# Four feed-forward networks on one core: another order of VectorE's adds and rests, and another order of work at the four entries

## The reference, cut to what matters

```
def swiglu_ffn(x, w_gate, w_up, w_down):
    return (jax.nn.silu(x @ w_gate) * (x @ w_up)) @ w_down
x = layer_norm(ALPHA * x + swiglu_ffn(x, ...), ln_ffn_g[l], ln_ffn_b[l])      # ffn0, ffn1

def sq_relu_mlp(h, w_up, w_down):
    u = jax.nn.relu(h @ w_up)
    return (u * u) @ w_down
h = h + sq_relu_mlp(rmsnorm(h, ln_mlp[layer]), w_up[layer], w_down[layer])    # mlp0, mlp1
```

## Time and profile before

| what | us |
|---|---|
| median of 3 runs | 2432.76 |
| the profiled execution, whole | 2433.45 |
| its span, first to last instruction | 2431.7 |
| TensorE busy | 2359.3 (97%) |
| VectorE busy | 1821.4 (75%) |
| ScalarE busy | 1144.4 (47%) |
| granted clock of TensorE, mean over the span | 0.991 of full speed |

### The profile page before, as it was taken

The page is one execution under the profiler, slowest core; times in us unless marked ns, Lnnn a source line. Parts: engine busy times, 40 slices in busy tenths (PEclk is TensorE's granted clock), DMA queues, the critical chain, the costliest instruction groups (busy, mean ns, idle before and its releaser), DMA issues.

```text
span 2431.7 us, 36017 instructions
## 1 busy us (share of the span) xinstructions
PE 2359.3 (97%) x13582; PEld 2023.7 (83%) x13582; DVE 1821.4 (75%) x2660; ACT 1144.4 (47%) x1846; POOL 24.8 (1%) x43
## 2 busy tenths in 40 slices
PE   8999999999999999999999999989999999899998
PEld 7887888899998887899998786778888777788887
DVE  6997646888777746888778636688888786888887
ACT  4455545444444744444445525444344565444443
POOL 0000000000000000000000000000000000000000
PEclk9999999999999999999999999999999999999999
DMA  5232313223223212223322220234422312223221
GB/s 182 104 139 87 121 35 104 89 102 103 103 89 147 97 43 70 93 98 103 103 93 102 87 104 18 88 100 121 120 97 99 122 53 70 71 102 103 99 91 70
DMA packets 39409, 232.56 MB, mean 96 GB/s; under 512 B 8901, under 2 KB 8981, under 8 KB 12560
## 3 DMA queue, kind: packets, MB, share of 16 engines
q1 hardware_dynamic: 31680, 219.17, 26.3%
q0 software_dynamic: 7632, 12.05, 1.7%
HBM read 223.80 MB, written 7.34 MB: 95 GB/s over the span
## 4 chain that ended last, share of the span: by engine, by line
PE 69%; DVE 17%; issue 8%; ACT 4%; DMA 1%; DVEq 1%; SPq 0%; ACTq 0%
PE bank L804 68%; DVE xs L2442 2%; DVE w_lo L2542 2%; DVE w_lo L2356 2%; DVE mhl L2595 2%; ACT w_hi L1651 1%; ACT xs L1732 1%; DMA w_raw<-weights_in 1%; ACT xh L1670 1%; DVE lox_y L2545 1%; DVE fhl L2595 1%; DVE tf_y L2628 1%; DVE cacc L2801 1%; DVE lox_x L2545 1%; PE bank L1582 1%
## 5 line engine op out<-in xcount | busy, mean ns | idle before, releaser
L804 PE MATMUL bank<-xh,w_hi 128*128 128x512 f32 (+1 forms) x1088 | 398.5, 366 | 22.9 <-DVE w_lo L2542 8.9
L804 PE MATMUL bank<-xh,w_lo 128*128 128x512 f32 (+1 forms) x1088 | 393.1, 361 | 0.0
L804 PE MATMUL bank<-xl,w_hi 128*128 128x512 f32 (+1 forms) x1088 | 393.1, 361 | 0.0
L2442 DVE TENSOR_TENSOR xs<-xs,bank 128x512 f32<-128x512 f32 x448 | 292.6, 679 | 38.8 <-PE bank L804 35.5
L2356 DVE TENSOR_TENSOR w_lo<-w_raw,w_hi 128x2048 fp32r<-128x2048 f32 x80 | 183.1, 2288 | 127.8 <-ACT w_hi L1651 127.7
L804 PEld LDWEIGHTS bank<-xh,w_hi 128*128 128x128 f32 x1088 | 208.2, 191 | 63.5 <-DVE w_lo L2542 9.8
L804 PEld LDWEIGHTS bank<-xl,w_hi 128*128 128x128 f32 x1088 | 208.7, 192 | 30.6 <-issue 0.5
L804 PEld LDWEIGHTS bank<-xh,w_lo 128*128 128x128 f32 x1088 | 208.4, 192 | 30.8
L804 PE MATMUL bank<-mhh,w_hi 128*128 128x512 f32 x512 | 204.7, 400 | 24.2 <-DVE mhl L2595 16.9
L2569 DVE TENSOR_TENSOR w_lo<-w_raw,w_hi 128x1024 fp32r<-128x1024 f32 x104 | 123.0, 1221 | 116.3 <-ACT w_hi L1798 116.3
L1810 ACT ACTIVATE rb<-bank 128x256 f32<-128x256 f32 x272 | 104.1, 383 | 220.0 <-PE bank L804 217.8
(11 more groups left out here) (383 smaller groups left out, 5781.1 us busy)
## 6 DMA issues: line engine op xcount, KB each, us to landing
w_raw<-weights_in SPq DMA_DIRECT2D x204, 1024.0 KB, 4.8
rel_scratch<-vt POOLq DMA_DIRECT2D x8, 384.0 KB, 19.4
bias<-rel_scratch POOLq DMA_DIRECT2D x8, 256.0 KB, 3.9
y_out<-xs SPq DMA_DIRECT2D x8, 256.0 KB, 2.2
xs<-x_in SPq DMA_DIRECT2D x3, 512.0 KB, 8.3
mk<-mem_in POOLq DMA_DIRECT2D x1, 1024.0 KB, 9.0
mem_kept<-memh POOLq DMA_DIRECT2D x1, 1024.0 KB, 4.3
mem_kept<-meml POOLq DMA_DIRECT2D x1, 1024.0 KB, 7.4
```

Source lines behind the costliest of these rows:

```text
L804: return pe.matmul(dst, a, b, start=start, stop=stop, skip_group_check=shared)
L2442: free(dve.tensor_tensor(xs[:, k, :], xs[:, k, :], bank(key)[:, :], ALU.add), key)
```

## The change

VectorE beside a down unit: each add goes ahead of the piece that it stood behind, adds 2 and 3 go ahead of piece 2, add 4 ahead of piece 3, the rests of the hidden chunk go behind piece 3, and in ffn the next unit's sums go behind adds 5 to 7. This runs in every call of beside_down.

At ffn's entry: the activation sums are made in the order in which seven uses them and split in that order, in between the pieces of gate 1; seven waits for each of them where it uses it; scale_residual goes to the end of the entry; the tile sums of gate 1 go ahead of pieces 1 to 3 of up 1, and ScalarE's order follows; the whole up unit goes to banks 4 and 5.

At mlp's entry: half_y is made by ScalarE straight behind the residual, ahead of the root; three of the four activation sums are made by VectorE ahead of the root and of unit 1's rests, the fourth behind these; the rests of two of the four and the sums of unit 3 go behind the rests of hidden chunk 0; the copy of the relative bias (L3205) and the wait for the root go into the entry, behind the sums.

```
@@ plan_banks: chunks
-            put(plain_up(name, "p0", "u", up_unit(name, 0), 2))
+            put(plain_up(name, "p0", "u", up_unit(name, 0), 4))
@@ TensorE: seven
                     if first:
-                        pe.wait_ge(sem["t_lo"], t_base[name] + 4)
+                        pe.wait_ge(sem["t_lo"], t_base[name] + 2)
                     free_bank("P2")
...
+                    if first:
+                        pe.wait_ge(sem["t_lo"], t_base[name] + 3)
                     product("R", r_[:, 0:MEM], of_unit(3), combined(2), start=True)
...
+                    if first:
+                        pe.wait_ge(sem["t_lo"], t_base[name] + 4)
                     product("P3", p_[:, 0:MEM], of_unit(2), combined(3))
@@ ScalarE
+            def scaled_tiles(gain):
+
+                for k in range(4):
+                    last = act.activation(half_y[:, k, :], xs[:, k, MEM:], ACT.Copy, scale=col(gain, k))
+                give(last, "scaled_half")
+
...
-                def combined_hi():
-
-                    for j in (0, 3, 1, 2):
+                def combined_hi(js=range(4)):
+
+                    for j in js:
...
-                    combined_hi()
+                    g1, u1 = gate_unit(name, 1), up_unit(name, 1)
+                    combined_hi((0, 1))
+                    quad(g1, 0)
+                    combined_hi((2, 3))
                     for m in range(2):
                         key = (name, "p0", "g", m)
                         drain(key, sil[:, m, :], bank(key)[:, :], ACT.Silu)
-                    for piece in range(4):
-                        quad(gate_unit(name, 1), piece)
+                    for piece in (1, 2, 3):
+                        quad(g1, piece)
+                    partial("p1", "g", "P1", 0)
+                    quad(u1, 0)
+                    partial("p1", "g", "Q1", 0)
                     for m in range(2):
                         hidden(0, m)
-                    beside_gate("p1", 1)
+                    partial("p1", "g", "P2", 0)
+                    quad(u1, 1)
+                    partial("p1", "g", "R", 0)
+                    for piece in (2, 3):
+                        quad(u1, piece)
+                    for m in range(2):
+                        silu("p1", 1, m)
...
             residual(pair_keys("go"), UNITS["go"], 4, None, gain="mlp2_g0")
+            scaled_tiles("mlp2_g0")
             rms_stats("r1")
@@ VectorE: sums_of_tokens (ffn) makes t1, t2, t4, t3 in this order; sums_of_scaled_tokens (mlp):
+                for j in js:
+                    if j == 0:
+                        g = COL[gain]
+                        steps.step(dve.tensor_scalar(ngain[:, :], prm[:, g:g + 4], -1.0, None, ALU.mult))
+                        steps.wait()
+                        seen.next("scaled_half")
+                        from_tiles(0, lambda k: xs[:, k, early], lambda k: ngain[:, k:k + 1], half, ALU.add)
...
+                    if j == 3:
+                        from_tiles(3, lambda k: xs[:, 4 + k, late], lambda k: col(gain, 4 + k), half, ALU.subtract)
@@ VectorE: beside_down
+                    adds(tag, (0,), i)
                     quad(n, 0, i)
-                    adds(tag, (0,), i)
+                    adds(tag, (1,), i)
                     quad(n, 1, i)
-                    rests(chunk, 0, i)
-                    adds(tag, (1,), i)
+                    adds(tag, (2, 3), i)
                     quad(n, 2, i)
-                    rests(chunk, 1, i)
-                    adds(tag, (2,), i)
+                    adds(tag, (4,), i)
                     quad(n, 3, i)
-                    adds(tag, (3, 4), i)
+                    for m in range(2):
+                        rests(chunk, m, i)
+                    adds(tag, (5, 6, 7), i)
                     if after is not None:
                         sums_of(after, i)
-                    adds(tag, (5, 6, 7), i)
@@ VectorE: entry of ffn
-                    combined_sums()
-                    sums_of(gate_unit(name, 1))
+                    g1, u1 = gate_unit(name, 1), up_unit(name, 1)
+                    sums_of_tokens()
+                    sums_of(g1)
+                    quad(g1, 0)
                     if name == "ffn0":
                         dve.wait_ge(mem_stored, 2 * 16)
-                    combined_lo()
-                    scale_residual()
-                    for piece in range(4):
-                        quad(gate_unit(name, 1), piece)
+                    combined_lo((0,))
+                    quad(g1, 1)
+                    combined_lo((1, 2))
+                    quad(g1, 2)
+                    quad(g1, 3)
+                    combined_lo((3,))
...
-                    sums_of(up_unit(name, 1))
+                    sums_of(u1)
+                    quad(u1, 0)
+                    sum_unit("p1", "g", 0)
+                    for piece in (1, 2, 3):
+                        quad(u1, piece)
                     for m in range(2):
                         rests(0, m)
-                    beside_gate("p1", 1)
+                    scale_residual()
@@ VectorE: entry of mlp
                     split_lo(U + 1)
-                    combined_sums()
-                    combined_lo()
+                    sums_of_scaled_tokens(gain, (3,))
+                    if name == "mlp0":
+                        key = ("vec", 0)
+                        wait_full(dve, key)
+                        free(dve.tensor_scalar(vt[0:16, 0:384], bank(key)[0:16, 0:384], -1.0, None, ALU.mult), key)
+                    combined_lo((0, 1))
+                    seen.next("rstd_ready")
                     first_hidden("p0", 0)
                     split_lo(U + 2)
-                    sums_of(up_unit(name, 2))
                     for m in range(2):
                         rests(0, m)
+                    combined_lo((2, 3))
+                    sums_of(up_unit(name, 2))
                     first_hidden("p1", 1)
...
             residual(pair_keys("go"), UNITS["go"], 4, False, gain="mlp2_g0")
-            key = ("vec", 0)
...
-            seen.next("rstd_ready")
+            sums_of_scaled_tokens("mlp2_g0", (0, 1, 2))
             chunks("mlp0", False)
```

More of the change, by code:

```diff
@@ L1901, in chunks @@
                     split_hi(U + 1)
[L1902 to L1905, removed]
                     combined_hi()
@@ L2327, in _ @@
             residual(pair_keys("so"), UNITS["so"], 4, None, first=1, gain="mlp2_g1")
+            scaled_tiles("mlp2_g1")
             rms_stats("r3")
@@ L2549, in quads_lo, with sums_of_tokens, sums_of_scaled_tokens, tile_of @@
                        .then_inc(w_lo_ready, 1)
+            def sums_of_tokens():
+                top, low = xs[:, 0:4, :], xs[:, 4:8, :]
+                t1, t2, t4, t3 = (tf_x[:, j, :].rearrange("p (k t) -> p k t", k=4) for j in range(4))
+                give(dve.tensor_tensor(t1, top[:, :, MEM:], top[:, :, 0:MEM], ALU.subtract), "t_ready")
+                own("t_ready")
+                give(dve.tensor_tensor(t2, low[:, :, MEM:], t1, ALU.subtract), "t_ready")
+                own("t_ready")
+                give(dve.tensor_tensor(t4, low[:, :, 0:MEM], t2, ALU.subtract), "t_ready")
+                give(dve.tensor_tensor(t3, low[:, :, MEM:], top[:, :, MEM:], ALU.subtract), "t_ready")
+            def sums_of_scaled_tokens(gain, js):
+                late, early = slice(MEM, T), slice(0, MEM)
+                def tile_of(j, k):
+                    return tf_y[:, j, k * MEM:(k + 1) * MEM]
+                def from_tiles(j, src, by, other, op):
+                    for k in range(4):
+                        last = dve.scalar_tensor_tensor(tile_of(j, k), src(k), by(k), other(k), ALU.mult, op)
+                    give(last, "t_ready")
+                def half(k):
+                    return half_y[:, k, :]
+                for j in js:
[5 more added lines that the diff above has]
+                        from_tiles(0, lambda k: xs[:, k, early], lambda k: ngain[:, k:k + 1], half, ALU.add)
+                    if j == 1:
+                        own("t_ready")
+                        from_tiles(1, lambda k: xs[:, 4 + k, late], lambda k: col(gain, 4 + k), lambda k: tile_of(0, k), ALU.subtract)
+                    if j == 2:
+                        own("t_ready")
+                        from_tiles(2, lambda k: xs[:, 4 + k, early], lambda k: col(gain, 4 + k), lambda k: tile_of(1, k), ALU.subtract)
+                    if j == 3:
+                        from_tiles(3, lambda k: xs[:, 4 + k, late], lambda k: col(gain, 4 + k), half, ALU.subtract)
             def chunks(name, has_mean):
@@ L2602, in product @@
                     dve.tensor_tensor(fh[:, m, :], fh[:, m, :], sil[:, m, :], ALU.mult).then_inc(sem["hf_ready"], 1)
[L2604 to L2638, removed]
@@ L2640, in combined_lo @@
-                def combined_lo():
-                    for j in (0, 3, 1, 2):
+                def combined_lo(js):
+                    for j in js:
                         seen.next("t_hi")
```

(15 more changed lines are left out.)

## The result

The changed kernel takes 2374.01 us (median of 4 runs, 2373.70 to 2374.26), the kernel before 2432.24 on the same chip; the ratio is 0.9761 with a 95% interval of 0.9744 to 0.9778. Forecast was 2375.0, in a range of 2369 to 2393. The profiled execution took 2374.26, its span is 2372.5, 59.2 under the span before, at a mean granted clock of 0.999.

> The changed kernel unedited, as the measure for the other three on the same chip: 2374.

A forecast was written before the change was run, and what follows sets the result against it. TensorE, busy 97% of the span, was taken as the bound. Loops 23.5, mlp entries 18.1 and ffn entries 16.2 sum to 57.8 us, taking the median from 2432.76 to 2375.0; range for 8 in 10: 2369 to 2393.

The forecast's parts named there:

- The order beside a down unit: Loops of ffn and mlp: the stall on add 2 goes in full, 42 x 0.56 = 23.5 us.
- slack at add 2: In the mlp step, add 2 was to be done 1.9 us before TensorE needs it, at 1659.7 against 1661.6.
- The rival that the stall moves: In the loops another add or piece becomes late and takes back up to 23.5 us: 2398.5; chance 0.07.
- The slow rival: Add 0, ahead of piece 0, waits for its tile and delays the pieces in 46 calls; 10 us gives 2486; chance 0.03.
- The entry of mlp: Entries of mlp0 and mlp1: VectorE's new order gains 9.9 and 8.2 us, together 18.1, bounds nothing to 23.
- TensorE does not wait: At mlp's entry, hidden rests end at 1576.1, so TensorE starts its first down unit at 1577.8 without a wait.
- 1.6 us of stalls at the adds: In mlp's first down unit, adds 0 to 2 come late: stalls of 0.8, 0.3, 0.2 and three restarts, 1.6 in sum.
- The entry of ffn: Entries of ffn0 and ffn1: the second gate seven starts 8.1 us earlier in each, together 16.2, bounds nothing to 18.
- in time by a hair: At ffn's entry, down weights' rests end at 456.7, up seven at 456.8; 0.2 us allowed for what this may cost.

The follow-up runs named there:

- the changed kernel's second: The changed kernel run unedited a second time, beside three of the experiments: 2374.42 us against 2432.80 for the kernel before, ratio 0.9759.
- sums late: The changed kernel with mlp's first three activation sums back behind the rests of unit 1, not ahead of the root: 2388.09 us, ratio 0.9813.
- fused chunks: The changed kernel with mlp's first two hidden chunks made by one operation per half, two tiny writes freeing the banks: 2371.16 us, ratio 0.9744.

## Why the prediction was right

*The order beside a down unit.* Right in mechanism, place and size. 0.56 per step was forecast, 0.58 measured: the four sets of adds are in time (slack at add 2 1.9 forecast, 2.0 read), nothing else became late, and the order alone gave it on the old entries. The rival that the stall moves is out by the trace: the adds' waits fell from 44 to 8, all in the first down units, and every later step lasts 20.98 or 31.06. The slow rival is out too: VectorE reaches add 0 at 1618.10 and works on without idle time. The granted clock did not fall in the first down units, to which the forecast had given 0.02, at 2418.7 us. The changed kernel has two short waits of weight loads in each of them, of 0.2 to 0.5 us, and its windows of 5 us over all four (460 to 470, 993 to 1003, 1555 to 1565, 2045 to 2055) read 1.00. The run with the wait moved has three within 4 us in mlp0's, at 1557.22, 1558.95 and 1560.69, and reads 1.00 from 1555 to 1565 too. In the kernel before, the windows over the later steps, with the 44 stalls in them, read 1.00 throughout (480 to 755, 1020 to 1290, 1605 to 1880, 2110 to 2385).

*The entry of mlp.* The sum was right (9.9 and 8.2 forecast, 9.9 and 8.3 measured). Of the 1.6 us by which the two differ, 1.4 is the kernel before's clock: behind 8.44 us of idle time in both networks the windows read 0.50 up to 1592 in mlp0 and up to 2097 in mlp1, and the down units lasted 13.84 and 12.41 us. One step was wrong in its working: "TensorE does not wait". The wait for the last two rests ahead of the loop was overlooked; they end at 1552.0 where TensorE was free at 1551.3. That it cost nothing was shown by moving it: what the start gained, the adds took back, as they hang on VectorE's chain alone. So the forecast's 1.6 us of stalls at the adds came as 1.2 at the start and 0.6 on the adds; with the wait moved, which is the kernel that the forecast had worked out, they came as 1.8 on the adds. That the overlooked wait fell into this gap was luck, not foresight. That chain as the bound was confirmed from both sides, by making it 1.2 us per hidden chunk shorter and by making it 5.0 longer.

*The entry of ffn.* Right to 0.1 us, with the down weights' rests "in time by a hair" read as 0.2 late, which the sum had allowed for. The waits for banks, pieces and rests that the forecast listed as in time all were. The bank and the scaling were shown to count by taking them back; for the rest of the new order there it is shown only that the entry as a whole gave what the sum said.

*What was off* lies in the experiments, not in the forecast: the price of an idle time of 3.9 us. The 3.7 per ffn expected for the old banks took the wait alone; the trace of before had already shown a clock of 0.50 behind 8.44 us and behind 4.46, there in the window printed with the result. In the sum, 57.8 forecast against 59.2, the difference is the 0.9 ahead of ffn0 and 0.9 more in the loops, less the 0.4 that went the other way. The 0.9 ahead of ffn0 remains without an edit that would explain it; the same kernel varies by as much there.

## What to carry to other kernels

Take the length of a stall from the distance between starts in a regular stretch, compare it with the due time of the one operation that ends it, and count the steps: 44 stalls of half a microsecond were as much as all the long waits. In an order written by hand, put first what the bound engine needs next and last what nobody waits for; write down each operation's end and its due time, since only the one with negative slack counts. And go through the bound engine's own list of waits line by line: one that was overlooked cost nothing here only because another stood right behind it.

## What the runs showed of the hardware

The price of an idle TensorE was not in proportion to its length. In the changed kernel the granted clock read 1.00 behind stalls of 0.2 to 1.1 us, behind one of 1.96 at 230.37, and behind the 6.44 ahead of the kernel's first matmul. The 1.96 stands in all 14 traces; in three of them (the kernel before, the changed kernel's second, the one with the old banks) the window 231 to 232 read 0.50, in the others 1.00. Behind 3.86 (old banks), 4.46 and 8.44 (kernel before), 6.23 and 6.37 (sums late) it read 0.50 (in the kernel before, behind 4.48 in ffn1, only from about 988.4 on: the first matmuls, from 987.49, start 0.12 apart, those from 988.49 on 0.21), with matmuls of 512 columns 0.43 us apart in place of 0.23. What the half clock cost on top of the wait was 1.4 and 1.5 us after 3.86, 1.9 and 2.1 after 6.23 and 6.37, and 2.9 and 1.5 after the two waits of 8.44 in the kernel before (first down units of 13.84 and 12.41 us against 10.91): two waits of one length differ more than a short and a long one.

Two tiny operations on VectorE cost next to nothing here. In the kernel with fused chunks the two writes of 128x1 that free the banks run beside the next subtraction, by their starts; at the second chunk, where an add follows them, it starts 0.2 us behind the end of the row before (1553.78, 1554.02). VectorE, timeline, start and length first:

```profile
1542.97 1.27 DVE L2706 SCALAR_TENSOR_TENSOR mh<-bank,rstd 128x512 f32<-128x512 f32 x2
1544.29 2.29 DVE L2376 TENSOR_TENSOR w_lo<-w_raw,w_hi 128x2048 fp32r<-128x2048 f32 x1
1544.31 0.07 DVE L2710 MEMSET ngain<- 128x1 f32 x2
```
